# Moving the norms' squares and sums between engines, filling TensorE's gaps, and splitting one weight block later, in a two-layer RG-LRU / GLA step

## The chip, the cores and the metric

The kernel runs on one core of a Trainium2 chip. The metric is the device time of one execution in microseconds (us). The engines are named as the profile names them: PE (TensorE, matmuls; PEld is its weight load), DVE (VectorE), ACT (ScalarE), POOL (GpSimd) and SP (SyncE, which here only issues DMAs). They run side by side and meet through semaphores.

## The reference, cut to what matters

Two groups of tokens (128 context tokens, 256 sample tokens; 384 in all) pass through two layers. Each layer is: half FFN, mixer (RG-LRU in layer 0, GLA in layer 1), half FFN. Each of these six stages begins with a modulated RMS norm, and a seventh norm ends the program:

```python
def rms_norm(x, g):
    y = xf * rsqrt(mean(xf * xf, axis=-1) + EPS)        # over 1024 features
    return y * g
def modulated(x, mod, gains, j):
    return rms_norm(x, gains[j]) * (1.0 + mod[3*j+1]) + mod[3*j]
def half_ffn(x, ...):                                   # w_in 1024 x 5632, w_out 2816 x 1024
    g, u = split(modulated(x, ...) @ w_in)
    return x + 0.5 * mod[3*j+2] * ((silu(g) * u) @ w_out)
# layer i: half_ffn, x += mod[5] * mixer(modulated(x)), half_ffn;   mod = silu(c) @ ada_w[i] + ada_b[i]
y = rms_norm(x, final_norm)
```

All is float32. The weights (some 250 MB) are read once.

## The kernel before, in words

**Layout.** x lies in SBUF as 8 chunks of 128 features (partitions) by 384 tokens. A matmul with float32 precision is made of three fp32r matmuls: high part of the weight by high part of the activation, high by low, low by high (L557 to L559 in `tile`). A weight block is up to 11 tiles of 128 x 128. It comes by DMA into `raw` (a ring of 4 slots, SP), ACT copies it to `w_hi_sb` (`hi_of`, L868), and DVE subtracts to get `w_lo_sb` (`lo_of`, L1242). `ahead(n)` does this for block n + 4. The semaphore `w_split` counts finished splits, and the load of block n + 4 into the slot waits for the split of block n.

**Stages.** `ffn_in` has 44 blocks of 8 tiles (24 matmuls each), `ffn_out` 16 blocks of 11 tiles (33 matmuls each, two blocks for one chunk of x), `rg_out` 8 blocks of 10 tiles, `gla_out` 8 blocks of 8 tiles. In the out stages, DVE adds each finished chunk to x (`update_x`, L1409, semaphore `x_ready`). In the FFN stages of the first three FFNs it also computes the modulation rows, called ada here: two multiply-and-sum passes over 128 x 1024 for each block of `ada_w` (L1261 and L1264), whose loads POOL issues into a ring of 2.

**A norm (q = 0 to 6).** While the stage before still runs, POOL squares chunks 0 to 6 of x and sums them into `ss` (`sum_squares`, L480 to L483). When chunk 7 is updated, ACT squares it into `sq_last` (L881) and loads the table for the square root (L882). PE sums over the partitions with `ones` as the moving operand, six matmuls with one column each (L575, L576), ACT takes the root (L884), DVE the reciprocal (L1293) and multiplies it with the identity into `diag` (L1294). PE multiplies `ones` with `diag`, which spreads the factor over all partitions (`rinv`, L584). Then for each chunk DVE scales (`scaled`, L1323), ACT adds the shift and rounds to the high part (L893), and DVE makes the low part (`low`, L1331).

**The start of a stage.** The first four blocks of a stage run in `arriving`: for chunks 0 to 4 all four blocks take the chunk as it arrives (8 matmuls with the high part, L595 and L596, then 4 with the low part, L599), and chunks 5 to 7 follow block by block. All four blocks must be split before the first matmul.

**The prologue.** SP loads small inputs, two pairs of ada blocks (1 MB each pair), all of x in one DMA, six more pairs, and the first four weight blocks. PE computes 7 of these 16 ada blocks, DVE 9. Then come norm 0, four `hi_of`, four `lo_of`, and the first stage. The masks for GLA are loaded from ACT's queue here.

The order of all of this is the order in which the code of each engine is written. There is no scheduler.

## Time and profile before

| | |
|---|---|
| median of 3 runs | 1612.21 us (1610.89 to 1615.01) |
| the profiled execution | 1613.05 us, of which the span from first to last instruction is 1611.4 us |
| busy share of the span | PE 94%, DVE 72%, ACT 39%, POOL 20% |
| mean granted TensorE clock | 0.970 of full |
| chain that ended last | PE 75%, DVE 11%, issue 5%, ACT 4%, POOL 3%, DMA 2% |

A row of the timeline is: start in us, duration in us, engine, line, operation, out<-in, shape, count, and in brackets the idle time before it and what ended it. Matmuls overlap, so that the time from one start to the next is what one costs.
### The profile page before, as it was taken

What the parts mean: (1) busy time and instruction counts of PE and PEld (TensorE: products, weight loads), DVE (VectorE), ACT (ScalarE), POOL (GpSimd) and SP (SyncE); (2) the same over time, 40 slices, a digit from 0 to 9 for tenths busy, and PEclk for the clock granted to TensorE, in tenths of its full rate; (3) what the DMA queues carried; (4) which work ended last, traced back from release to release, by engine and by line L of the source; (5) the groups of instructions that cost most, each with busy time, mean ns of one, the idle gap of its engine ahead of it and who ended that gap; (6) DMA issues with size and microseconds to landing.
All of it is one profiled execution on the core that took longest, in us unless ns stands there. A gap on an engine that the chain in (4) does not pass through costs nothing.

```text
span 1611.4 us, 24129 instructions
## 1 busy us (share of the span) xinstructions
PE 1520.8 (94%) x8554; PEld 1490.4 (92%) x8554; DVE 1164.8 (72%) x1691; ACT 634.7 (39%) x883; POOL 325.4 (20%) x377
## 2 busy tenths in 40 slices
PE   6899999989978999999899999989989889999997
PEld 5899999979978999999899999989779789999997
DVE  6898889878987777789977777986766665434432
ACT  1533342259973333332333333225444444333321
POOL 5010002300244000014200000321567240000031
PEclk9999999989988999999899999999999899999998
DMA  8476676513423556666455556652212133333421
GB/s 335 168 245 232 212 248 220 197 59 105 148 69 131 192 186 195 199 212 235 161 171 194 186 197 209 220 209 66 92 65 80 40 105 119 129 128 130 158 92 39
DMA packets 67909, 257.00 MB, mean 159 GB/s; under 512 B 7537, under 2 KB 8561, under 8 KB 67473
## 3 DMA queue, kind: packets, MB, share of 16 engines
q1 hardware_dynamic: 48512, 187.57, 34.0%
q0 software_dynamic: 18432, 67.12, 12.6%
q10 hardware_dynamic: 912, 1.65, 0.3%
q8 instruction: 28, 0.46, 0.1%
q14 instruction: 25, 0.20, 0.0%
HBM read 253.68 MB, written 2.63 MB: 159 GB/s over the span
## 4 chain that ended last, share of the span: by engine, by line
PE 75%; DVE 11%; issue 5%; ACT 4%; POOL 3%; DMA 2%; SPq 0%; DVEq 0%; ACTq 0%; POOLq 0%
PE bank L557 21%; PE bank L559 21%; PE bank L558 21%; DVE wide L1261 3%; DVE wide L1264 3%; PE bank L595 2%; PE bank L596 2%; PE bank L599 2%; ACT w_hi_sb L868 1%; PE wide L766 1%; DMA ada_raw<-in_ada_w 1%; DVE w_lo_sb L1242 1%; DMA x<-in_x 1%; DVE x L1409 1%; POOL scr L483 1%
## 5 line engine op out<-in xcount | busy, mean ns | idle before, releaser
L868 ACT ACTIVATE w_hi_sb<-raw 128x1024 fp32r<-128x1024 f32 (+3 forms) x308 | 344.1, 1122 | 535.4 <-PE bank L559 524.6
L557 PE MATMUL bank<-h_hi,w_hi_sb 128*128 128x384 f32 x1620 | 546.7, 337 | 3.8 <-DVEq L1804 3.0
L1242 DVE TENSOR_TENSOR w_lo_sb<-raw,w_hi_sb 128x1024 fp32r<-128x1024 f32 (+3 forms) x308 | 427.0, 1388 | 168.3 <-ACT w_hi_sb L868 163.9
L559 PE MATMUL bank<-h_hi,w_lo_sb 128*128 128x384 f32 x1620 | 544.9, 336 | 0.0
L558 PE MATMUL bank<-h_lo,w_hi_sb 128*128 128x384 f32 x1620 | 544.9, 336 | 0.0
L557 PEld LDWEIGHTS bank<-h_hi,w_hi_sb 128*128 128x128 f32 x1620 | 305.1, 188 | 6.3 <-DVEq L1804 3.2
L558 PEld LDWEIGHTS bank<-h_lo,w_hi_sb 128*128 128x128 f32 x1620 | 305.1, 188 | 0.1
L559 PEld LDWEIGHTS bank<-h_hi,w_lo_sb 128*128 128x128 f32 x1620 | 305.0, 188 | 0.0
L557 PE MATMUL bank<-a_hi,w_hi_sb 128*128 128x384 f32 x704 | 237.0, 337 | 2.5 <-DVE a_lo L1390 1.5
L559 PE MATMUL bank<-a_hi,w_lo_sb 128*128 128x384 f32 x704 | 236.6, 336 | 0.0
L558 PE MATMUL bank<-a_lo,w_hi_sb 128*128 128x384 f32 x704 | 236.6, 336 | 0.0
L1261 DVE CUSTOM_DVE_ANT_0 wide<-ada_raw,extra 128x1024 f32<-128x1024 f32 x128 | 171.8, 1342 | 8.1 <-DMA ada_raw<-in_ada_w 7.8
L1264 DVE CUSTOM_DVE_ANT_0 wide<-ada_raw,extra 128x1024 f32<-128x1024 f32 x128 | 157.8, 1233 | 4.4
L458 POOL DMA_DIRECT2D ada_raw<-in_ada_w x80 | 42.6, 532 | 553.0 <-DVE mod_turn L1264 508.0
L557 PEld LDWEIGHTS bank<-a_hi,w_hi_sb 128*128 128x128 f32 x704 | 132.3, 188 | 3.7 <-issue 3.7
L558 PEld LDWEIGHTS bank<-a_lo,w_hi_sb 128*128 128x128 f32 x704 | 132.4, 188 | 0.0
L559 PEld LDWEIGHTS bank<-a_hi,w_lo_sb 128*128 128x128 f32 x704 | 132.4, 188 | 0.0
L910 ACT ACTIVATE tmp_b<-bank 128x384 f32<-128x384 f32 x88 | 43.2, 491 | 207.8 <-PE bank L559 207.8
L1379 DVE TENSOR_TENSOR tmp_a<-tmp_b,bank 128x384 f32<-128x384 f32 x88 | 48.8, 555 | 100.7 <-PE bank L559 97.9
L483 POOL TENSOR_TENSOR scr<-scr 128x384 f32<-128x384 f32 x42 | 77.4, 1843 | 3.3
L595 PE MATMUL bank<-h_hi,w_hi_sb 128*128 128x384 f32 x140 | 54.7, 391 | 14.8 <-ACT h_hi L893 14.8
L465 POOL DMA_DIRECT2D ada_raw<-in_ada_w x48 | 26.5, 552 | 171.0 <-DVE mod_all L1264 164.9
(263 smaller groups left out, 1616.3 us busy)
## 6 DMA issues: line engine op xcount, KB each, us to landing
raw<-in_ffn_in SPq DMA_DIRECT2D x176, 512.0 KB, 3.6
ada_raw<-in_ada_w POOLq DMA_DIRECT2D x128, 512.0 KB, 3.6
raw<-in_ffn_out SPq DMA_DIRECT2D x64, 704.0 KB, 4.2
...
```

The source lines that it names most:

```text
L458: pool.dma_start(ada_raw[:, b, :], d["ada_w"][bass.ds(ADA_RING * i + (first + b), 1)].rearrange("a p k -> p (a k)")).then_inc(ada_loaded[b ...
L483: add = nc.gpsimd.tensor_tensor(ss[:, :], ss[:, :], sq[:, :], ALU.add)
L557: pe.matmul(out, w_hi_sb[:, slot, w], hi[k], start=start and j == 0, stop=False)
L558: pe.matmul(out, w_hi_sb[:, slot, w], lo[k], start=False, stop=False)
L559: last = pe.matmul(out, w_lo_sb[:, slot, w], hi[k], start=False, stop=stop and j == len(ks) - 1)
L595: pe.matmul(bank[b][:, 0:T], w_hi_sb[:, b, w], chunks[0][k], start=k == 0, stop=False)
L868: A(w_hi_sb[:, s, 0:w], raw[:, s, 0:w], ACT.Copy).then_inc(w_hi, 1)
L910: A(tmp_b[:, p, 0:T], bank[2 * p][:, 0:T], ACT.Silu).then_inc(silu_ready, 1)
L1242: V.tensor_tensor(w_lo_sb[:, s, 0:w], raw[:, s, 0:w], w_hi_sb[:, s, 0:w].bitcast(F32), ALU.subtract).then_inc(w_split, 1)
L1261: V.tensor_tensor_reduce(wide[:, :], w, crow[:, 0, :], 1.0, 0.0, ALU.mult, ALU.add, accum_out=out[:, 0:1]).then_inc(ada_half, 1)
L1264: V.tensor_tensor_reduce(wide[:, :], w, crow[:, 1, :], 1.0, 0.0, ALU.mult, ALU.add, accum_out=out[:, 1:2]).then_inc(done, 1)
L1379: V.tensor_tensor(tmp_a[:, two, :], tmp_b[:, two, :], bank[2 * two + 1][:, 0:T], ALU.mult).then_inc(drained, 2)
```

## The change

Eight things change.

- The squares of chunks 0 to 6 move from POOL to ACT (`square`), and the additions into `ss` move to DVE (`add_square`). In an FFN's out stage ACT squares chunk m after it has split block 2m + 5, and DVE adds after the same block's low part. POOL keeps only its DMA issues and the work inside the mixers.
- The column sums come in two parts: three matmuls with `ss` before the wait for `sq_last`, three behind it.
- `diag` is gone. PE takes the factor itself, broadcast along columns, as the stationary operand and the identity as the moving one (three matmuls of 128 columns, fp32).
- `keep_busy(n)`: n matmuls of `ones` by `ident` into an unused bank, whose result nobody reads. There are 4 before the second part of the sums, 5 behind it, and 9 behind the spreading, the 9 not in norms 0 and 6, and none at all in norm 0.
- The table of the root is loaded before the wait for chunk 7.
- The last of the four first blocks of a stage is split inside the norm, behind chunk 4 (`LATE`), and `arriving` runs three blocks by chunks (chunks 0 to 6), then the fourth as a whole.
- Prologue: x comes in 8 pieces, one behind each pair of ada blocks, the masks behind the fourth piece and on SP's queue; ACT makes three of the four high parts before the root; DVE makes the first low part before the reciprocal and two behind it.
- POOL issues its 16 ada loads of an out stage in one run. `wg2` is loaded behind norm 4's last chunk.

```diff
 def sum_squares(q, loads=None):                       # POOL: all of it is removed
-    ...
@@ TensorE
+def keep_busy(n):
+    for _ in range(n):
+        pe.matmul(bank[7][:, 0:P], ones[:, :], ident, start=True, stop=True)
 def norm_sums(q):
-    pe.wait_ge(ss_ready, q + 1)
+    pe.wait_ge(sq_added, (DC - 2) * (q + 1))
     ...
+    for t in range(NT):
+        pe.matmul(sum_ps[:, t:t + 1], ss[:, t * P:(t + 1) * P], ones[:, 0:1], start=t == 0, stop=False)
+    if q:
+        keep_busy(4)
     pe.wait_ge(sq_ready, q + 1)
     for t in range(NT):
-        pe.matmul(sum_ps[:, t:t + 1], ss[:, tok], ones[:, 0:1], start=True, stop=False)
         last = pe.matmul(sum_ps[:, t:t + 1], sq_last[...], ones[:, 0:1], ...)
 def norm(q):
     if q:
         norm_sums(q)
-    pe.wait_ge(diag_ready, q + 1)
-    pe.matmul(rinv, ones[:, :], diag[...], start=True, stop=True).then_inc(rinv_ready, 1)
+        keep_busy(5)
+    pe.wait_ge(factor_ready, q + 1)
+    for t in range(NT):
+        last = pe.matmul(rinv[:, t * P:(t + 1) * P], rstd[:, t:t + 1].to_broadcast([P, P]), ident, ...)
+    last.then_inc(rinv_ready, 1)
+    if 0 < q < 6:
+        keep_busy(9)
-def arriving(base, ks, chunks, hi_ready, ready, n0, early=5, bank=bank):
+def arriving(base, ks, chunks, hi_ready, ready, n0, early=5, bank=bank, together=RING):
     ...                                               # RING -> together in all loops
+    for b in range(together, RING):
+        pe.wait_ge(w_split, base + b + 1)
+        tile(bank[b][:, 0:T], b, ks, *chunks, True, True).then_inc(w_used, 1)
-    one_tile_blocks(f"ffn_in{f}", ..., DC * q)
+    one_tile_blocks(f"ffn_in{f}", ..., DC * q, DC - 1, RING - 1)       # also rg and gla_qk
@@ ScalarE
 def norm_stats(q):
     ...
+    nc.scalar.preload_act_table_set("sqrt_and_others")
+    if q:
         act.wait_ge(x_ready, DC * q)
     A(sq_last[:, :], x[:, DC - 1, :], ACT.Square).then_inc(sq_ready, 1)
-    nc.scalar.preload_act_table_set("sqrt_and_others")
+    if q == 0:
+        for n in range(RING - 1):
+            hi_of(n)
 def norm_apply(q, tables):
     ...
+        if q and m == LATE:
+            ahead(BASE[STAGE_BEFORE[q]] + COUNT[STAGE_BEFORE[q]] - 1)
+        if q == 0 and m == LATE:
+            hi_of(RING - 1)
-def only_weights(name):
-    for b in range(COUNT[name]):
+def only_weights(name, q=None, per=1):
+    for b in range(COUNT[name] - 1):
         ahead(BASE[name] + b)
+        if q and b % per == per - 1 and b // per < DC - 1:
+            square(q, b // per)
@@ VectorE
 def norm_stats(q):
-    seq.step(V.reciprocal(rstd[:, 0:NT], rstd[:, 0:NT]))
-    V.tensor_tensor(diag[:, :, :], ident..., rstd..., ALU.mult).then_inc(diag_ready, 1)
+    V.reciprocal(rstd[:, 0:NT], rstd[:, 0:NT]).then_inc(factor_ready, 1)
+def add_square(q, m):
+    dve.wait_ge(sq_made, (DC - 1) * q + m + 1)
+    if m > 1:
+        dve.wait_ge(sq_added, (DC - 2) * q + m - 1)
+    V.tensor_tensor(ss[:, :], ss[:, :], sq[:, :], ALU.add).then_inc(sq_added, 1)
@@ SyncE, prologue
 for s in range(ADA_START // 2):
-    if s == 2:
-        sp.dma_start(x[:, :, :], d["x"]).then_inc(x_loaded, 16)
     sp.dma_start(ada_first[:, 2 * s:2 * s + 2, :], ...)
+    sp.dma_start(x[:, s, :], d["x"][:, s, :]).then_inc(x_loaded[s], 16)
+    if s == 3:
+        sp.dma_start(mask_in, d["masks"]).then_inc(masks_loaded, 16)
```

How the order on the engines changes is shown at three places. The first is PE between the last matmul of `ffn_out0` and the first of the mixer (norm 1); `scr` is the buffer that holds `ss`, `sq_last` and `diag`, and `small` holds the identity. Before:

```order
L559 MATMUL bank<-a_hi,w_lo_sb 128x384
L619 REGISTER_ALU
L619 COMPARE_AND_BRANCH
L575 MATMUL bank<-ones,scr 128x1
L576 MATMUL bank<-ones,scr 128x1
L575 MATMUL bank<-ones,scr 128x1
L576 MATMUL bank<-ones,scr 128x1
L575 MATMUL bank<-ones,scr 128x1
L576 MATMUL bank<-ones,scr 128x1
L584 MATMUL bank<-scr,ones 128x384
L595 MATMUL bank<-h_hi,w_hi_sb 128x384
```

And the same place in the changed kernel:

```order
L537 MATMUL bank<-a_hi,w_lo_sb 128x384
L613 REGISTER_ALU
L613 COMPARE_AND_BRANCH
L556 MATMUL bank<-ones,scr 128x1 x3
L548 MATMUL bank<-small,ones 128x128 x4
L561 MATMUL bank<-ones,scr 128x1 x3
L548 MATMUL bank<-small,ones 128x128 x5
L572 MATMUL bank<-small,rstd 128x128 x3
L548 MATMUL bank<-small,ones 128x128 x9
L586 MATMUL bank<-h_hi,w_hi_sb 128x384
```

The sums stand in two groups, and 18 matmuls that nobody waits for are queued between the steps of the norm.

The second place is DVE inside norm 3 of the changed kernel, around chunk 4 (L1336 scales, L1344 makes the low part, L1258 is the low part of a weight block):

```order
L1344 SCALAR_TENSOR_TENSOR h_lo<-tmp_a,mod_all,h_hi 128x128
L1344 SCALAR_TENSOR_TENSOR h_lo<-tmp_a,mod_all,h_hi 128x256
L1258 TENSOR_TENSOR w_lo_sb<-raw,w_hi_sb 128x1024
L1336 SCALAR_TENSOR_TENSOR tmp_a<-x,gain,bank 128x128
L1336 SCALAR_TENSOR_TENSOR tmp_a<-x,gain,bank 128x256
L1344 SCALAR_TENSOR_TENSOR h_lo<-tmp_a,mod_all,h_hi 128x128
L1344 SCALAR_TENSOR_TENSOR h_lo<-tmp_a,mod_all,h_hi 128x256
```

Before, that low part of a weight block stood ahead of the reciprocal, and the chunks followed one another without it.

The third place is DVE in `ffn_out1`, behind the update of a chunk (L1433 updates x, L1277 is an ada pass), in the changed kernel:

```order
L1433 SCALAR_TENSOR_TENSOR x<-bank,halfgate,x 128x128
L1433 SCALAR_TENSOR_TENSOR x<-bank,halfgate,x 128x256
L1258 TENSOR_TENSOR w_lo_sb<-raw,w_hi_sb 128x1024
L1428 TENSOR_TENSOR scr<-scr 128x384
L1277 ISA wide,mod_all<-ada_raw,extra 128x1024
```

The addition of a chunk's squares (L1428) is new there, between the low part and the ada pass.

## Rows read from the trace of the kernel before

**Rows 1.** Stretches: us, busy time (count) by engine, granted clock, DMA share, GB/s

```profile
0.00:49.80 49.80, 28.39 (x126) 27.10 (x126) 35.20 (x50) 12.67 (x16) 22.50 (x23) 1.00 0.82 316
...
22.00:26.00 4.00, 4.00 (x20) 4.00 (x20) 3.82 (x5) 0.00 (x0) 3.83 (x3) 1.00 1.03 410
...
503.70:511.60 7.90, 3.20 (x16) 2.03 (x15) 4.32 (x11) 5.28 (x8) 0.00 (x0) 0.69 0.64 228
1077.10:1088.60 11.50, 4.56 (x17) 3.17 (x15) 6.70 (x17) 5.60 (x9) 0.00 (x0) 0.63 0.53 194
1088.60:1314.80 226.20, 208.87 (x1168) 191.89 (x1168) 151.98 (x217) 103.24 (x166) 110.33 (x133) 0.94 0.23 75
```

**Rows 2.** Timeline across norm 2, PE, ACT and DVE

```profile
503.75 0.74 DVE L1409 SCALAR_TENSOR_TENSOR x<-bank,mod_all,x 128x128 f32<-128x128 f32 x2 [2.40 <-PE bank L559]
...
504.77 0.51 ACT L881 ACTIVATE scr<-x 128x384 f32<-128x384 f32 x1
...
505.29 1.28 ACT L882 ACT_TABLE_LOAD   x1
505.42 0.35 PE L575 MATMUL bank<-ones,scr 128*128 128x1 f32 x2 [1.71 <-ACT scr L881]
...
506.97 0.26 ACT L884 ACTIVATE rstd<-bank,eps 128x3 f32<-128x3 f32 x1 [0.40 <-PE bank L576]
...
507.48 0.56 DVE L1294 TENSOR_TENSOR scr<-small,rstd 128x384 f32<-128x384 f32 x1
...
508.09 1.65 PE L584 MATMUL bank<-scr,ones 128*128 128x384 f32 x2 [1.16 <-DVE scr L1294]
509.85 1.39 DVE L1323 SCALAR_TENSOR_TENSOR tmp_a<-x,gain,bank 128x128 f32<-128x128 f32 x4 [1.73 <-PE bank L584]
...
511.57 0.66 PE L595 MATMUL bank<-h_hi,w_hi_sb 128*128 128x384 f32 x1 [1.83 <-ACT h_hi L893]
```

**Rows 3.** Timeline, PE inside GLA: six fp32 matmuls of 128 columns, two passes each

```profile
1205.84 1.50 PE L766 MATMUL wide<-ebuf 128*128 128x128 f32 x12
```

**Rows 4.** First matmul of a stage to the clock's rise, first of five and sum

```profile
335.10:339.90 4.80, 4.79 (x16) 4.80 (x17) 4.69 (x14) 2.63 (x8) 0.00 (x0) 0.55 0.02 3
...
sum 26.30, PE 26.25 PEld 26.29 DVE 25.70 ACT 14.73 POOL 0.00; mean PE 5.25 PEld 5.26 DVE 5.14 ACT 2.95 POOL 0.00
```

**Rows 5.** Timeline, DVE: low parts of two chunks in norm 2, one in norm 4

```profile
514.33 0.74 DVE L1331 SCALAR_TENSOR_TENSOR h_lo<-tmp_a,mod_all,h_hi 128x128 fp32r<-128x128 f32 x2
...
515.76 0.74 DVE L1331 SCALAR_TENSOR_TENSOR h_lo<-tmp_a,mod_all,h_hi 128x128 fp32r<-128x128 f32 x2
...
1090.13 0.97 DVE L1331 SCALAR_TENSOR_TENSOR h_lo<-tmp_a,mod_all,h_hi 128x128 fp32r<-128x128 f32 x2
```

**Rows 6.** Timeline, DVE in the out stage of the third FFN

```profile
1049.66 2.42 DVE L1242 TENSOR_TENSOR w_lo_sb<-raw,w_hi_sb 128x1408 fp32r<-128x1408 f32 x1 [0.15 <-DVE x L1409]
1052.01 2.04 DVE L1261 CUSTOM_DVE_ANT_0 wide<-ada_raw,extra 128x1024 f32<-128x1024 f32 x1
...
1055.29 1.62 DVE L1242 TENSOR_TENSOR w_lo_sb<-raw,w_hi_sb 128x1408 fp32r<-128x1408 f32 x1
...
1079.18 0.74 DVE L1409 SCALAR_TENSOR_TENSOR x<-bank,halfgate,x 128x128 f32<-128x128 f32 x2
```

**Rows 7.** Groups of instructions: busy us, mean ns of one, idle before

```profile
L1390 DVE TENSOR_TENSOR a_lo<-tmp_a,a_hi 128x384 f32 x80 | 44.3, 554 | 0.0
```

**Rows 8.** Timeline of the prologue, DVE

```profile
9.29 1.23 DVE L1261 CUSTOM_DVE_ANT_0 wide<-ada_first,extra 128x1024 f32<-128x1024 f32 x1 [9.29 <-DMA ada_first<-in_ada_w]
...
21.29 1.73 DVE L1261 CUSTOM_DVE_ANT_0 wide<-ada_first,extra 128x1024 f32<-128x1024 f32 x1
...
40.67 1.23 DVE L1264 CUSTOM_DVE_ANT_0 wide<-ada_first,extra 128x1024 f32<-128x1024 f32 x1
...
43.58 4.63 DVE L1242 TENSOR_TENSOR w_lo_sb<-raw,w_hi_sb 128x1024 fp32r<-128x1024 f32 x4
...
48.13 1.38 DVE L1323 SCALAR_TENSOR_TENSOR tmp_a<-x,gain,bank 128x128 f32<-128x128 f32 x4
```

136 lines of the change are left out of this document (67 added, 69 removed).

## The prediction, made before the changed kernel was run

> **What bounds the kernel now.** I read the engines' shares first: PE is busy for 94% of the span, so the kernel is one stream of matmuls with holes. The table of stretches shows where the holes are. The first 49.8 us hold no matmul of a stage [rows 1], and between two stages PE's weight matmuls pause for some 8 us five times (7.9 us at norm 2), with 11.5 us at norm 4 [rows 1]; a seventh pause ends the program. Third, the timeline across one norm shows the pause as a chain over three engines [rows 2]: x's last chunk, ACT's square, PE's sums, root, reciprocal, diagonal, spreading, scaling, first matmul. Nothing there is throughput. Fourth, the granted clock: it is 0.69 over that pause [rows 1] and still 0.55 in the first 4.8 us of the stage behind norm 1 [rows 4]. So each pause costs twice, once as waiting and once as matmuls at 1.2 GHz. Inside the stages PE hardly waits; what DVE, ACT and POOL do there is free unless it is late at the stage's end.
>
> **The chain of a norm, by norm 2** [rows 2].
> - ACT starts the last square at 504.77, since a `hi_of` stands before it; x is ready at 503.75 + 0.74 = 504.49. Without the `hi_of` it starts at 504.54: 0.23 us earlier, at 504.54, done at 505.05.
> - The sums: six matmuls from 505.42, root at 506.97, so 1.55 us. A matmul here is two passes, and two passes of one column last 0.22 us in start-to-start time (twelve passes in 1.44). Three of the six go before the wait. Behind it stand 0.66 us, so 0.67 to 0.9 us are saved; I take 0.89.
> - What stands before the wait must not be late: 3 sums (0.66) and 4 fillers. One fp32 matmul of 128 columns costs 2 x (1.50 - 0.27)/11 = 0.22 us at full clock [rows 3]; together 1.55 us from 503.54, so PE is free at 505.1, and the square reaches PE at 505.2. They fit, by 0.1 us.
> - The root and the reciprocal take 0.11 + 0.26 + 0.04 + 0.18 us. The diagonal (0.56 us and a hand-over) goes: 0.6 us saved. But 5 fillers (1.1 us) are queued behind the sums, in front of the spreading, and the factor is there after about 0.7 us. So 0.4 us of the gain are given back.
> - The spreading cost 1.65 us, at the low clock. Three matmuls of 128 columns are 6 x 0.111 + 0.17 = 0.83 us at full clock: 0.8 us saved (at half clock 1.45: 0.2 saved).
> - From scaling to first matmul 1.72 us, unchanged; 9 fillers (2.0 us from the spreading's last issue) end at about the same moment.
> Sum: 0.23 + 0.89 + 0.6 - 0.4 + 0.8 = 2.1 us; going through the times one by one gives 2.0. Norms 3 and 5 have the same chain, norm 1 slightly slower sums: 2.4, 2.0, 1.9 us for norms 1, 2, 5.
>
> **DVE's lateness.** Norm 4's pause is 11.5 us because DVE updates the last chunk only at 1079.18 [rows 6], 2 us after PE's last matmul at 1077.1. In that stage a POOL tensor instruction makes DVE's pass of 1.62 us last 2.42 and its pass of 1.23 us last 2.04 [rows 6, 8]: 1.6 us for each chunk. That goes; an addition of 0.55 us [rows 7] comes, with ACT's square finished beneath the low part. So DVE wins 1.0 us for each of seven chunks and is on time: about 1.7 us at norm 4 and 0.3 to 0.5 at norm 3. Norm 4's chain gives 3.3 more, since its pause is so long that six sums run at the low clock (0.43 us each, 1.2 us more than at norm 2). I take 5.0 at norm 4 and 2.3 at norm 3. ACT's seven squares of 0.51 us lie beneath PE in a stage where ACT is busy for a third. Bound on the other side: if the additions made DVE wait for ACT by 1 us each, DVE would be as late as now and 2 us of this are lost.
>
> **The end.** Norm 6 has the same chain without the last fillers: 0.7 + 0.6 - 0.4 + 0.8 = 1.6 us.
>
> **The clock.** Five stages begin with 26.3 us in all at a granted clock near 0.54 [rows 4], 16 matmuls in the first of them and 88 in the five, that would take 0.173 us each at full clock (15.2 us): 11.1 us lost. If the fillers keep the clock up, this is gained. But then PE can be faster than the chunks arrive. Three blocks take 9 x 0.173 = 1.56 us a chunk; DVE delivers one in 1.43 us [rows 5] and so stays ahead, until the late low part (1.23 us) comes in behind chunk 4. Following both engines chunk by chunk I get waits of 0.3 us at chunk 5 and 0.4 at chunk 7: 0.7 us. In norm 4 the chunks are rearranged, a low part takes 0.97 instead of 0.74 [rows 5], a chunk 1.65, which is slower than PE's 1.56: some 2.6 us of waits. 4 x 0.7 + 2.6 = 5.4 us come off: net 5.7 us. Before, with four blocks (2.08 us a chunk), DVE never was the limit.
>
> The bounds of this term: 11.1 us from above, and from below the case where the clock falls all the same (rival 1). The rows show that PE at work is not enough: within norm 2 the pieces of idle time are 1.7, 1.2 and 1.8 us with sums between them, and the clock falls. The sums move one column each. A filler moves 128 columns in two passes back to back, like GLA's matmuls, in whose stage the granted clock is 0.94 [rows 1]. So I take "held".
>
> The table load before the root ends at 505.29 + 1.28 = 506.57 [rows 2], before the sums do; it costs nothing now, and would be 0.4 us late behind the shorter sums if it were not moved. The Trainium skill (ScalarE: Activation LUTs, "What ACT_TABLE_LOAD costs") gives a load with its drain as 2.66 us. By that the root could not have begun before 507.95, and moving it would win 1.0 us more per norm, 6 us in all. The trace does not agree: the root begins at 506.97. The measurement decides, and this is no part of the sum.
>
> **The prologue** [rows 1, 8]. DVE starts its 9 ada blocks at 9.3 and is through at 41.9, with one wait for the transfer of all of x. With POOL at work one pass lasts 1.73 instead of 1.23 us. Now a block costs two passes with their readout, 2 x 1.38 = 2.76 us, and six additions 0.6 us each with their hand-over: 9 x 2.76 + 3.6 = 28.4, so 37.8. The DMA keeps up: 410 GB/s bring a pair of blocks and a piece of x (1.25 MB) in 3.04 us against DVE's 3.36; the last pair lands near 31.6, the last piece of x at 32.1. ACT has squared it and made three high parts (1.06 us each, the third when its load lands, near 36) by 37.1, the root by 37.4. DVE makes one low part (1.16 us), reciprocal, mods, gain, two low parts, and starts scaling at 42.4 instead of 48.13: 5.7 us. The fourth low part is hidden, as PE starts at the low clock. Before, this first stage ran only 3.4 us at the low clock until it rose; the other five took 5.3 on average [rows 4]. I count the average here, 1.9 us more at the low clock, of which almost half is lost: 0.9 to 1.0 us. 4.7 us net, between 3 (DMA pieces of 1.5 KB rows slower than before, by no row) and 6.5.
>
> **The sum.** Prologue 4.7; chains 2.4 + 2.0 + 2.3 + 5.0 + 1.9 + 1.6 = 15.2; clock 5.7: 25.6 us. From the profiled execution's 1613.05: 1587.4. The median is 0.84 lower; 1587.
>
> **Rivals.**
> 1. The clock falls in the pauses all the same. Then the fillers cost double: 5 of them 2.1 us against 0.7 needed, 9 of them 3.8 against 1.7, so 3.6 us of overrun against 1.7 us saved. But 9 fillers and the spreading are continuous work just ahead of the stage, and the clock comes back earlier, by up to the 2.2 us that a stage loses now. The five norms together give nothing, except DVE's 2 us at norms 3 and 4; with the prologue and norm 6: 1606. If it falls in two or three of five: 1597. For it: the fit before the second sums has a margin of 0.1 us only, and PE is idle or in one-column work for 1.3 of each pause. Against: the 18 fillers are 4 us of the 6 us.
> 2. DVE's chunk chain starves PE more than I follow, since each hand-over between ACT and DVE behind the late block is exposed: 1.5 us more at five stages, 1594 to 1595. For it: 1.43 against 1.56 us is a thin lead.
> 3. Slower than before: the fillers themselves. If the clock falls and the 9 fillers do not bring it back, each of five pauses is 1.9 us longer (9.5), the stages begin as cold as now, and only the prologue and norm 6 are won (5.7 together); if the small DMAs of x and DVE's later additions take the prologue's gain too, nothing stands against 9.5: 1613 to 1621. It decides from the point where the clock is low in all five pauses when the second group of fillers starts.
> 4. The additions hold DVE up in the out stages. Only norms 3 and 4 could tell: 2 us less, inside the range.
>
> **How the numbers follow.** Forecast as worked out 0.70; rival 1 0.15, of which a third beyond 1605; rival 2 0.10; rival 3 0.05. Likeliest 1587, its own range 1582 to 1592. The range reaches to partly lost clocks: 1579 to 1600. About 0.3% (4.8 us) can be told from no change. Faster by more: 0.70 + 0.10 + 0.12 = 0.92; within: 0.05; slower: 0.03.
>
> **What would show it.** Scaling of norm 0 at 42.4. Each pause, last matmul to first weight matmul, near 6 us, norm 4's 6.5. Granted clock 1.00 there and no 0.32 us matmul spacing behind. PE waits of below 1 us behind chunk 4, more in norm 4. DVE's passes all at 1.23 and 1.62 us in the out stages, x's last chunk 0.4 us behind PE at norm 4. Wrong would be: a clock of 0.5 at any stage start, PE busy with fillers when `rstd` has long been ready, or a longer wait of PE for `w_lo_sb` of the fourth block.

## The result and the profile after

| | median of the runs | profiled span | mean granted clock | PE busy |
|---|---|---|---|---|
| before | 1612.56 us (1610.89 to 1615.01, 4 runs) | 1611.4 us | 0.970 | 94% |
| changed | 1586.07 us (1584.52 to 1588.69, 4 runs) | 1585.4 us | 0.987 | 96% |

The ratio is 0.9834, with a 95% interval from 0.9820 to 0.9848: 26 us faster. The prediction was 1587 us.

The stretches of the changed kernel (columns as in [rows 1]: length, then busy time and count of PE, PEld, DVE, ACT and POOL, then granted clock, DMA share and GB/s): prologue, first stage, pause of norm 1, RG-LRU stage, pause of norm 2, pause of norm 4.

```profile
0.00:44.10 44.10, 28.32 (x130) 27.98 (x131) 31.06 (x54) 15.04 (x21) 2.15 (x10) 1.00 0.89 345
44.10:321.40 277.30, 276.80 (x1584) 276.50 (x1585) 239.32 (x364) 99.98 (x132) 24.38 (x46) 1.00 0.63 217
321.40:327.50 6.10, 6.10 (x55) 6.08 (x54) 2.38 (x8) 2.86 (x6) 0.00 (x0) 1.00 0.00 0
327.50:492.70 165.20, 150.99 (x843) 148.34 (x843) 144.75 (x244) 132.64 (x204) 31.99 (x32) 0.96 0.36 118
492.70:498.90 6.20, 6.20 (x56) 6.18 (x55) 2.45 (x9) 2.99 (x6) 0.00 (x0) 1.00 0.05 19
...
1061.00:1067.50 6.50, 6.43 (x57) 6.25 (x55) 2.86 (x11) 3.28 (x7) 0.00 (x0) 1.00 0.00 1
```

Beside [rows 1], the pause of norm 2 is 6.2 us with PE busy throughout at a granted clock of 1.00; it was 7.9 us with 3.2 us of work at 0.69. The pause of norm 4 went from 11.5 to 6.5 us. One row is misleading. The granted clock also says 1.00 for the first stage, although its first matmuls start 0.32 us apart, against 0.173 us at full clock; there, in the first microseconds of the program, the distance of the starts is the better witness.

The timeline across norm 2, to be set beside [rows 2]:

```profile
493.02 0.74 DVE L1433 SCALAR_TENSOR_TENSOR x<-bank,mod_all,x 128x128 f32<-128x128 f32 x2 [2.35 <-PE bank L537]
493.41 1.14 PE L548 MATMUL bank<-small,ones 128*128 128x128 f32 x8
493.80 0.52 ACT L881 ACTIVATE scr<-x 128x384 f32<-128x384 f32 x1 [3.14 <-DVE x L1433]
494.38 0.82 PE L561 MATMUL bank<-ones,scr 128*128 128x1 f32 x6
495.07 1.36 PE L548 MATMUL bank<-small,ones 128*128 128x128 f32 x10
495.24 0.26 ACT L886 ACTIVATE rstd<-bank,eps 128x3 f32<-128x3 f32 x1 [0.92 <-PE bank L561]
...
495.54 0.18 DVE L1309 RECIPROCAL rstd<-rstd 128x3 f32<-128x3 f32 x1 [1.77 <-ACT rstd L886]
...
496.26 0.83 PE L572 MATMUL bank<-small,rstd 128*128 128x128 f32 x6
```

ACT squares 0.04 us after x is there, the sums behind the square take 0.82 us (three matmuls) instead of 1.55 (six), the spreading 0.83 instead of 1.65. No PE row has an idle time in brackets: the fillers (L548; x8 is four of them, two passes each) close the gaps. They also hold the spreading up. The reciprocal starts at 495.54 and takes 0.18 us, and PE comes to L572 only at 496.26, behind five fillers (L548, x10).

Set out by the first and last weight matmul of each stage, the 26.0 us of span are:

| | before | after | won |
|---|---|---|---|
| first matmul of the first stage | 49.84 | 44.11 | 5.7 |
| pauses of norms 1 to 5 | 8.70, 8.20, 8.46, 11.62, 8.08 | 6.28, 6.28, 6.27, 6.53, 6.21 | 13.5 |
| from the last weight matmul to the end | 12.83 | 11.22 | 1.6 |
| stages 1 to 6 | 276.57, 168.26, 277.71, 279.23, 225.88, 276.02 | 277.26, 165.00, 275.61, 280.15, 225.65, 274.83 | 5.2 |

### The profile page after: what moved, and what is told of

The parts are those of the page before. It is cut to its first block, busy times and chain, and to the rows that moved or that the text cites. A ratio compares the mean times of both kernels' runs of the same rounds, so it can differ in the third digit from the quotient of the medians.

```text
span 1585.4 us, 24611 instructions
## 1 busy us (share of the span) xinstructions
PE 1525.6 (96%) x8780; PEld 1501.9 (95%) x8780; DVE 1139.2 (72%) x1726; ACT 655.5 (41%) x932; POOL 193.4 (12%) x286
## 4 chain that ended last, share of the span: by engine, by line
PE 85%; DVE 5%; ACT 3%; POOL 2%; issue 2%; DMA 2%; SPq 1%; POOLq 0%; DVEq 0%; ACTq 0%
PE bank L535 25%; PE bank L537 24%; PE bank L536 24%; PE bank L586 1%; PE bank L587 1%; PE bank L590 1%; PE bank L548 1%; DMA ada_first<-in_ada_w 1%; PE wide L759 1%; ACT w_hi_sb L861 1%; DMA ada_raw<-in_ada_w 1%; DVE w_lo_sb L1258 1%; POOL ebuf L523 1%; DVE wide L1280 1%; DVE wide L1277 1%
## 5 line engine op out<-in xcount | busy, mean ns | idle before, releaser
L1258 DVE TENSOR_TENSOR w_lo_sb<-raw,w_hi_sb 128x1024 fp32r<-128x1024 f32 (+3 forms) x308 | 404.4, 1314 | 170.0 <-ACT w_hi_sb L861 166.7
L1277 DVE CUSTOM_DVE_ANT_0 wide<-ada_raw,extra 128x1024 f32<-128x1024 f32 x128 | 157.1, 1227 | 9.4 <-DMA ada_raw<-in_ada_w 9.1
L1280 DVE CUSTOM_DVE_ANT_0 wide<-ada_raw,extra 128x1024 f32<-128x1024 f32 x128 | 157.8, 1233 | 4.4
L463 POOL DMA_DIRECT2D ada_raw<-in_ada_w x80 | 42.6, 533 | 604.5 <-DVE mod_turn L1280 523.2
L926 ACT ACTIVATE a_hi<-tmp_a 128x384 f32 (+1 forms) x88 | 45.2, 513 | 30.1 <-DVE tmp_a L1396 30.1
L895 ACT ACTIVATE h_hi<-tmp_a,mod_all 128x128 fp32r<-128x128 f32 x96 | 39.6, 468 | 34.4 <-DVE tmp_a L1336 34.4
```

Source lines behind the costliest of these rows:

```text
L463: pool.dma_start(ada_raw[:, b, :], d["ada_w"][bass.ds(ADA_RING * i + (first + b), 1)].rearrange("a p k -> p (a k)")).then_inc(ada_loaded[b ...
L926: A(out, tmp_a[:, p, 0:T], ACT.Copy).then_inc(ahi_ready, 1)
L1258: V.tensor_tensor(w_lo_sb[:, s, 0:w], raw[:, s, 0:w], w_hi_sb[:, s, 0:w].bitcast(F32), ALU.subtract).then_inc(w_split, 1)
L1277: V.tensor_tensor_reduce(wide[:, :], w, crow[:, 0, :], 1.0, 0.0, ALU.mult, ALU.add, accum_out=out[:, 0:1]).then_inc(ada_half, 1)
L1280: V.tensor_tensor_reduce(wide[:, :], w, crow[:, 1, :], 1.0, 0.0, ALU.mult, ALU.add, accum_out=out[:, 1:2]).then_inc(done, 1)
```

## The experiments

The median of the kernel before, run beside them, was 1612.51 us for no_fill, together4, pool_loop and pool_squares, 1611.56 for the next four rows and 1613.31 for the last four. The pauses and the length of the third stage (us) are from one execution, the profiled one, of each; a pause goes from the start of the last weight matmul to the start of the next stage's first, a stage from its first to its last.

| | median (range, runs) | ratio to before, 95% interval | pauses of norms 1 to 5 | 3rd stage |
|---|---|---|---|---|
| changed kernel | 1586.07 (1584.5 to 1588.7, 4) | 0.9834 (0.9820 to 0.9848) | 6.28 6.28 6.27 6.53 6.21 | 275.61 |
| no_fill | 1592.50 (1590.6 to 1594.5, 4) | 0.9870 (0.9852 to 0.9887) | 5.88 5.88 5.87 6.84 5.80 | 277.55 |
| together4 | 1614.78 (1605.3 to 1619.1, 12) | 1.0007 (0.9990 to 1.0024) | 7.93 9.56 9.55 8.18 9.49 | 277.51 |
| pool_loop | 1585.90 (1582.5 to 1586.7, 5) | 0.9827 (0.9812 to 0.9842) | 6.27 6.29 6.27 6.53 6.22 | 275.61 |
| pool_squares | 1587.99 (1585.6 to 1593.2, 5) | 0.9840 (0.9826 to 0.9854) | 6.28 6.28 6.26 9.69 6.21 | 275.62 |
| together4_by5 | 1599.15 (1596.0 to 1603.7, 6) | 0.9920 (0.9906 to 0.9935) | 7.93 7.93 11.02 8.18 9.49 | 275.24 |
| mid_by7 | 1595.12 (1594.7 to 1599.8, 4) | 0.9892 (0.9878 to 0.9906) | 6.21 6.21 6.24 6.70 6.22 | 277.51 |
| mid_by5 | 1583.96 (1580.7 to 1589.7, 5) | 0.9826 (0.9808 to 0.9845) | 6.21 6.22 6.24 6.69 6.21 | 275.24 |
| with_diag | 1585.60 (1583.7 to 1587.4, 5) | 0.9836 (0.9824 to 0.9849) | 6.46 6.46 6.46 6.71 6.39 | 275.61 |
| fill3 | 1584.39 (1581.9 to 1586.8, 5) | 0.9817 (0.9804 to 0.9831) | 5.89 5.89 5.89 6.14 5.82 | 275.61 |
| warm0 | 1584.36 (1582.7 to 1586.8, 5) | 0.9819 (0.9806 to 0.9832) | 6.28 6.28 6.28 6.54 6.21 | 275.61 |
| first_four | 1589.64 (1584.2 to 1594.2, 5) | 0.9843 (0.9824 to 0.9861) | 6.29 6.29 6.27 6.53 6.21 | 275.59 |
| combined | 1582.43 (1579.0 to 1583.0, 5) | 0.9806 (0.9792 to 0.9819) | 6.02 6.02 6.25 6.69 5.82 | 275.22 |

**no_fill: the fillers alone taken out.**

```diff
-                for _ in range(n):
+                for _ in range(0):
                     pe.matmul(bank[7][:, 0:P], ones[:, :], ident, start=True, stop=True)
```

> The changed kernel without its fillers (keep_busy issues nothing); all else as changed. Theory A (the fillers hold TensorE's clock, and that is worth what the stages' starts lost before): the granted clock falls to 0.5 in all five pauses between stages, the spreading of the factor costs 1.45 instead of 0.83 us, but starts up to 0.4 us earlier; the five stages begin at the low clock as in the kernel before, about 11 us lost there, less the waits behind the late split (they vanish under slow matmuls, about 3 us). Time 1586 + 8 = 1592 to 1596, ratio to the kernel before 0.987 to 0.990. Rival B (the split sums and the shorter chain alone keep the pause short enough): clock stays at 1.0, the 0.4 us that the second group of fillers holds up each norm come back: 1584, ratio 0.982.

Measured 1592.5 us, 6.4 above the changed kernel. The first 4.6 us of the third stage, and below them the pause of norm 2 that stands before it:

```profile
502.60:507.20 4.60, 4.56 (x14) 4.59 (x15) 4.49 (x14) 2.44 (x7) 0.00 (x0) 0.50 0.01 4
496.80:502.60 5.80, 2.62 (x20) 2.25 (x18) 2.44 (x9) 2.97 (x6) 0.00 (x0) 0.85 0.04 18
```

The pause is 0.40 us shorter without fillers, but the clock falls inside it, and the stage's first 4.6 us run at 0.50. The third stage is 1.9 us longer (277.55 against 275.61), the last one 2.3. So at such a norm the fillers cost 0.4 us and bring about 2. The intervals of the two ratios do not touch. The stretch of the changed kernel behind the same norm shows that it held:

```profile
498.90:511.40 12.50, 12.46 (x72) 12.05 (x72) 10.85 (x29) 6.62 (x16) 0.00 (x0) 1.00 0.13 43
```

**together4: the late split undone in norms 1 to 5, fillers kept.** All four first blocks run chunk by chunk up to the seventh chunk.

```diff
-                arriving(..., DC - 1, bank, RING - 1)         # norms 1 to 5
+                arriving(..., DC - 1, bank, RING)
-                    if q and m == LATE:
-                        ahead(BASE[STAGE_BEFORE[q]] + COUNT[STAGE_BEFORE[q]] - 1)
-                for b in range(COUNT[name] - 1):              # and the same for DVE
+                for b in range(COUNT[name]):
```

> The changed kernel with the late split undone in norms 1 to 5: all four first blocks are split before the norm, and the four take each chunk together (as before, chunks 0 to 6 together); fillers kept. Norm 0 keeps its late split. Theory A (with the clock up, the late low part makes TensorE wait for chunks, so the late split costs time): TensorE needs 2.08 us a chunk against DVE's 1.43 and never waits; 0.8 us come back at norms 1 to 3 and 5 and 2.2 at norm 4, against 0.23 to 0.28 us that ACT's extra high part delays the last square at each of five norms: net 3 us faster, 1583, ratio 0.9815. Rival B (the late split is worth more than it costs, since a high part in front of the last square moves the whole chain and shifts it against the fillers): 1587 to 1589, ratio 0.985.

Measured 1614.78 us: all of the gain gone, and every theory's number missed by 25 us or more. The profile shows two faults. The first is in the pause, here of norm 2:

```profile
501.18 0.74 DVE L1429 SCALAR_TENSOR_TENSOR x<-bank,mod_all,x 128x128 f32<-128x128 f32 x2 [2.35 <-PE bank L537]
501.24 1.06 ACT L861 ACTIVATE w_hi_sb<-raw 128x1024 fp32r<-128x1024 f32 x1 [3.73 <-PE bank L537]
...
502.32 1.28 ACT L878 ACT_TABLE_LOAD   x1
...
503.61 0.52 ACT L881 ACTIVATE scr<-x 128x384 f32<-128x384 f32 x1
504.19 0.83 PE L561 MATMUL bank<-ones,scr 128*128 128x1 f32 x6 [1.48 <-ACT scr L881]
504.88 2.45 PE L548 MATMUL bank<-small,ones 128*128 128x128 f32 x10
```

The copy of the last block must wait for PE's last matmul, and the table load and the last square are queued behind it on ACT. The square starts at 503.61, 1.69 us after x is there, instead of 0.04. PE is idle for 1.48 us, the clock falls, and the ten passes of five fillers take 2.45 us instead of 1.36, in front of the spreading. So a filler can also do harm: once the clock is low it costs twice, on the chain. The late split is not there for DVE alone; it is what lets the table load stand ahead of x's last chunk. The second fault comes some 20 us behind four of the five pauses (not behind norm 4's), and the next runs take it apart. The pauses of the profiled execution, one of the faster of the twelve with 1609.9 us, add up to 13.1 us more than the changed kernel's; where the slower ones lost 5 us more is not known.

Here the Trainium skill can be weighed (ScalarE: Activation LUTs, "What ACT_TABLE_LOAD costs": 2.66 us with the drain). In these rows the load starts when the copy ends and takes 1.28 us, and the square starts 1.29 us after the load's start. The trace does not agree with the longer figure here.

**together4_by5, mid_by7, mid_by5: the two faults apart.** together4_by5 keeps the copy where together4 has it. `by5` lets the chunk-by-chunk part end at the fifth chunk, as before the change. `mid` splits the last block in the pause, but behind the last square on ACT and behind the reciprocal on DVE.

```diff
-                arriving(..., DC - 1, bank, RING - 1)
+                arriving(..., 5, bank, RING)                 # by5; DC - 1 in by7
                 A(sq_last[:, :], x[:, DC - 1, :], ACT.Square).then_inc(sq_ready, 1)
+                if 0 < q < 6:                                # mid; DVE alike, ahead of norm_apply
+                    ahead(BASE[STAGE_BEFORE[q]] + COUNT[STAGE_BEFORE[q]] - 1)
```

> The four first weight blocks together as in the run before last (together4, 1614.8 us), but chunk by chunk only up to the fifth chunk of h, the last three chunks block by block, as the kernel before had it. Theory S (slots): with all four blocks taken chunk by chunk up to the seventh, their slots come free only at the end and within 2 us of each other, so the fifth block's halves (ACT 1.06 us, then DVE 1.23 us) are late; that is the wait of 2.3 to 2.7 us for w_lo_sb behind each of the five pauses, with a half-speed stretch behind it. Here these waits vanish, and the pauses stay at 7.9 to 9.6 us because the fourth block's copy by ACT is still queued ahead of the table load and the last square: 1598 to 1603 us. Rival R: the stages are longer because they start cold behind the longer pauses, and the waits are a consequence: 1611 to 1615.

> The last block of a stage is split in the pause itself, but out of the way: ACT copies it behind the last square, DVE takes its low part behind the reciprocal; then four blocks chunk by chunk up to the seventh. Theory Q (queue) says that the pauses' extra 1.65 to 3.3 us in together4 came from the copy ahead of the table load and the last square, so they are 6.3 to 6.5 us here. Theory S says that the wait for the fifth block's low part (2.3 to 2.7 us, five times) stays: 1595 to 1604 us. If four blocks by seven chunks were harmless in themselves: 1583 to 1586.

> As mid_by7, with the chunk-by-chunk part up to the fifth chunk only. Q and S together: pauses of 6.3 to 6.5 us, no wait for the fifth block, and no wait for h_lo behind a late split (1.2 us at norm 4); against that up to 1 us a norm where PE is at the sixth chunk ahead of DVE (4 x 5 x 3 x 0.173 = 10.4 us of work against 8 chunks at 1.44). 1584 to 1589 us, that is: the changed kernel's time without its late split. If the late split of three blocks is needed in itself: over 1592.

| third stage / pause before it | up to chunk 7 | up to chunk 5 |
|---|---|---|
| copy ahead of the square | 277.51 / 9.56 | 275.24 / 7.93 |
| copy behind the square | 277.51 / 6.21 | 275.24 / 6.22 |

The medians landed where both theories together put them, mid_by5 at the edge (1583.96, 1584 to 1589 expected). The number of chunks sets the stage. The place of the copy sets the pause, but by how much hangs on the clock. Where it holds, the copy ahead of the square costs 1.65 us: 7.93 against 6.28, and 8.18 against 6.53 at norm 4. Where it falls, copy and clock together cost 3.3 us, and 4.8 at norm 3 in together4_by5 (11.02, above the 9.6 that I expected). Norm 2 in together4_by5 has the same 1.48 us of idle time as in together4, and its fillers run at full clock:

```profile
498.96 0.83 PE L561 MATMUL bank<-ones,scr 128*128 128x1 f32 x6 [1.48 <-ACT scr L881]
499.65 1.36 PE L548 MATMUL bank<-small,ones 128*128 128x128 f32 x10
```

So 9.56 against 7.93 in the first row of the table is the clock, and not the chunks. The second fault in mid_by7, behind norm 2:

```profile
519.74 0.49 ACT L916 ACTIVATE tmp_b<-bank 128x384 f32<-128x384 f32 x1 [5.95 <-PE bank L537]
520.13 1.99 ACT L861 ACTIVATE w_hi_sb<-raw 128x1024 fp32r<-128x1024 f32 x2
521.21 1.23 DVE L1258 TENSOR_TENSOR w_lo_sb<-raw,w_hi_sb 128x1024 fp32r<-128x1024 f32 x1 [6.64 <-ACT w_hi_sb L861]
522.57 0.56 DVE L1396 TENSOR_TENSOR tmp_a<-tmp_b,bank 128x384 f32<-128x384 f32 x1
...
523.26 0.44 PE L535 MATMUL bank<-h_hi,w_hi_sb 128*128 128x384 f32 x1 [2.00 <-DVE tmp_a L1396]
```

ACT had been idle for 5.95 us and DVE for 6.64, since no block was finished; then four finish within some 2 us, and PE waits for what the two must do with the first: a split into its slot, and the emptying of its bank. PE waited for `tmp_a` behind norms 2, 3 and 5 (2.0 us each), for `w_lo_sb` behind norm 1 (2.7 us), and for neither behind norm 4: four waits, not the five of the expectation. In the changed kernel the held-back fourth block is PE's work in that time. My expectation named the slot alone; the banks are as much of it.

mid_by5 has neither fault nor a late split. Its third stage is 0.37 us shorter than the changed kernel's, its last 0.34. The first 96 weight matmuls of a stage are its four first blocks. The time from the first to the last of them shows the cost where it arises, apart from what happens later in the stage:

| first 96 weight matmuls, us | behind norm 1 | 2 | 3 | 4 | 5 |
|---|---|---|---|---|---|
| changed (three blocks by 7 chunks, late split) | 16.93 | 16.93 | 16.93 | 18.60 | 16.91 |
| mid_by5 (four blocks by 5 chunks) | 16.57 | 16.56 | 16.56 | 18.16 | 16.57 |
| mid_by7 (four blocks by 7 chunks) | 16.57 | 16.55 | 16.55 | 16.56 | 16.57 |

Without any wait they take 16.56 us. So beside mid_by5 the late split costs 0.34 to 0.37 us, and 0.44 behind norm 4. Behind norm 4, where DVE's chunks come more slowly [rows 5], mid_by5 loses 1.6 us as well, though I had expected no such wait there:

```profile
1077.98 0.44 PE L535 MATMUL bank<-h_hi,w_hi_sb 128*128 128x384 f32 x1 [1.31 <-DVE h_lo L1346]
```

The median of mid_by5, 1583.96, is not distinguishable from 1586.07.

**pool_squares: squares and sums of norms 1 to 6 back on POOL.**

```diff
+                    seq.step(nc.gpsimd.tensor_tensor(sq[:, :], x[:, m, :], x[:, m, :], ALU.mult))
+                    nc.gpsimd.tensor_tensor(ss[:, :], ss[:, :], sq[:, :], ALU.add).then_inc(sq_added, 1)
...
-                        square(q, b // per)                  # ACT
-                        add_square(norm_q, b)                # DVE
```

> The changed kernel with squares and sums of norms 1 to 6 back on POOL as before (norm 0 stays on ACT and DVE), its ada loads interleaved as before; split sums, fillers, spreading and late split kept. Theory A (moving the squares only matters by POOL slowing DVE): passes of DVE beside POOL last 2.04 instead of 1.23 us and 2.42 instead of 1.62, DVE updates the last chunk 2 us late at norm 4 and 0.5 us at norm 3, nothing at the others: 2 to 3 us slower than the changed kernel, 1588 to 1589, ratio 0.985 to 0.9855; with the pause longer by 2 us at norm 4, the clock may fall there and take 2 us more, 1591. Rival B (POOL's sums are late for the first part of the column sums, at every norm): 1 us or more at each of six norms, 1593 or more. Rival C: no difference, 1586.

The median, 1587.99, is where theory A had it, but the intervals overlap, and it cannot be told from the changed kernel's. The pauses can: only norm 4's changes, 9.69 us instead of 6.53, and DVE's low parts in the stage before it are long again. From pool_squares, then from the changed kernel:

```profile
1046.22 2.43 DVE L1274 TENSOR_TENSOR w_lo_sb<-raw,w_hi_sb 128x1408 fp32r<-128x1408 f32 x1 [0.15 <-DVE x L1449]
...
1065.20 0.74 DVE L1449 SCALAR_TENSOR_TENSOR x<-bank,halfgate,x 128x128 f32<-128x128 f32 x2
```

```profile
1039.92 1.62 DVE L1258 TENSOR_TENSOR w_lo_sb<-raw,w_hi_sb 128x1408 fp32r<-128x1408 f32 x1 [0.73 <-ACT w_hi_sb L861]
...
1061.33 0.74 DVE L1433 SCALAR_TENSOR_TENSOR x<-bank,halfgate,x 128x128 f32<-128x128 f32 x2 [0.82 <-PE bank L537]
```

The last update has no wait in the first: DVE is late, 2.23 us behind the start of PE's last matmul instead of 0.38. In the second it waits for PE. That is 1.85 of the 3.16 us. The rest is the clock, which falls here behind 1.68 us of idle time and makes the spreading and the nine fillers slow (0.67 and 0.61 us), as the expectation had allowed for:

```profile
1066.55 0.83 PE L579 MATMUL bank<-ones,scr 128*128 128x1 f32 x6 [1.68 <-ACT scr L899]
...
1068.46 1.49 PE L590 MATMUL bank<-small,rstd 128*128 128x128 f32 x6
```

At norm 3 nothing is seen (6.26 against 6.27). In the kernel before, DVE was 0.92 us behind PE there, in pool_squares it waits for PE. So POOL's squares alone do not bring that lateness back, and what took it away stays open.

**with_diag: the factor spread as before the change** (reciprocals on a diagonal by DVE, one matmul of 384 columns), fillers kept.

```diff
+                V.tensor_tensor(diag[:, :, :], ident..., rstd[:, 0:NT]..., ALU.mult).then_inc(factor_ready, 1)
-                for t in range(NT):
-                    last = pe.matmul(rinv[:, t * P:(t + 1) * P], rstd[:, t:t + 1].to_broadcast([P, P]), ident, ...)
+                pe.matmul(rinv, ones[:, :], diag..., start=True, stop=True).then_inc(rinv_ready, 1)
```

> The factor is spread as before the change: DVE puts the reciprocals on a diagonal (0.56 us in the kernel before) and one matmul of 384 columns with ones spreads it, instead of three of 128 columns with the identity; all fillers stay. Theory: the diagonal lies on the chain, so each of six pauses is 0.4 to 0.6 us longer, 2.4 to 3.6 us in all: 1588.5 to 1590. Rival: PE is held by its ten fillers for most of that time anyway (they end 0.7 us behind the reciprocal), so only 0.1 to 0.2 us a pause is seen: 1586.5 to 1587.5.

The rival was right: pauses of 6.46 instead of 6.28, and a median of 1585.60 us that cannot be told from the changed kernel's. The step that took 0.56 us on DVE [rows 2] is hidden, but for 0.18 us, behind the five fillers. In norm 0, which has none, the same step costs 0.6 us: from the start of the last sum to the spreading it is 3.73 against 3.14 us.

**fill3: three fillers instead of five ahead of the spreading.**

```diff
-                    keep_busy(5)
+                    keep_busy(3)
```

> Five keep-alive matmuls of 128 columns behind the first part of the column sums become three. The five take 1.14 us on PE and end 0.1 to 0.4 us behind the last square of ACT, which the second part of the sums waits for. Theory: each pause is 0.3 to 0.4 us shorter (6.28 to 5.9) and the clock still holds: 1584 to 1585 us, which a median may not tell from the changed kernel; the pauses tell it. Rival: with two fillers fewer the clock falls in the pause and the stage starts at half speed, 1 to 2 us a stage: 1590 to 1595.

(The expectation puts the five behind the first part of the sums; they stand behind the second.) The pauses are 5.89 us, as short as with no fillers at all, and the stages as long as with five (275.61, 274.85), so the clock held. The median, 1584.39 us, cannot be told from the changed kernel's (the intervals overlap); the pauses and stages show the 0.39 us a norm.

**warm0: twelve fillers in norm 0.**

```diff
+                else:
+                    keep_busy(6, 3)            # ahead of the spreading, in bank 3
...
+                if q == 0:
+                    keep_busy(6, 3)            # behind it
```

> Norm 0, which has no fillers in the changed kernel, gets six ahead of and six behind the spreading of the factor (into a bank that is free there), in the two stretches of 2.79 and 2.80 us in which PE waits. The changed kernel's first stage runs 4.5 us at half clock (44.11 to 48.58). Theory: the clock is up at or soon behind the start, and 1 to 2.2 us are won: 1584 to 1585 us, the first stage 275.1 to 276.3 us long instead of 277.3. Rival: at half clock twelve fillers take 0.44 us each, delay the spreading or the first matmul, and the clock still rises only with the stage: 1586 to 1588, the stage as long as now.

All but its first matmul start at the spacing of the full clock, and the stage is 275.61 us long instead of 277.26, as the first theory said:

```profile
45.84 0.42 PE L590 MATMUL bank<-h_hi,w_hi_sb 128*128 128x384 f32 x1 [2.08 <-ACT h_hi L899]
46.09 0.34 PE L591 MATMUL bank<-h_hi,w_lo_sb 128*128 128x384 f32 x1
46.27 0.33 PE L590 MATMUL bank<-h_hi,w_hi_sb 128*128 128x384 f32 x1
```

In the changed kernel the same matmuls start 0.32 us apart:

```profile
44.57 0.53 PE L587 MATMUL bank<-h_hi,w_lo_sb 128*128 128x384 f32 x1
44.89 0.53 PE L586 MATMUL bank<-h_hi,w_hi_sb 128*128 128x384 f32 x1
45.21 0.53 PE L587 MATMUL bank<-h_hi,w_lo_sb 128*128 128x384 f32 x1
```

The start itself, 45.84, is 1.7 us later in this execution. The loads of the prologue come in at different times: with an unchanged prologue the start lay between 44.11 (changed) and 45.27 (pool_squares) in nine kernels. That the fillers do not hold it up is seen in combined, which has the same twelve and starts at 44.42. The medians do not decide here.

**first_four: the first stage's late split undone.**

```diff
-                    for n in range(RING - 1):
+                    for n in range(RING):
                         hi_of(n)
-            for b in range(1, RING - 1):
+            for b in range(1, RING):
                 lo_of(b)
```

> The first stage's late split undone: ACT and DVE split all four first weight blocks ahead of norm 0's scaling, and PE takes four blocks chunk by chunk up to the fifth chunk of h; the rest of the prologue's change stays. Theory: DVE has one low part more (1.15 us) on the chain, so the scaling starts at 43.5 to 43.7 us from the span's start instead of 42.40, and of this 0.5 to 0.7 comes back because the first stage then loses no 0.7 us to the late split (277.3 us long, 276.6 before the change): 1586 to 1587.5 us. Rival: the 0.7 us is not the split's but the half clock's (4.5 us of it instead of 3.3), so the stage stays 277.3 us long and the whole 1.15 is lost: 1587 to 1588.

From the reciprocal to the scaling it is 4.49 us instead of 2.96, and the root before it is late as well. The DVE rows, of first_four and then of the changed kernel:

```profile
41.01 3.50 DVE L1256 TENSOR_TENSOR w_lo_sb<-raw,w_hi_sb 128x1024 fp32r<-128x1024 f32 x3
44.42 1.38 DVE L1334 SCALAR_TENSOR_TENSOR tmp_a<-x,gain,bank 128x128 f32<-128x128 f32 x4
```

```profile
40.12 2.36 DVE L1258 TENSOR_TENSOR w_lo_sb<-raw,w_hi_sb 128x1024 fp32r<-128x1024 f32 x2
42.40 1.38 DVE L1336 SCALAR_TENSOR_TENSOR tmp_a<-x,gain,bank 128x128 f32<-128x128 f32 x4
```

The scaling starts 2.0 us later, more than both theories gave it. The low part is 1.14 us of this. The rest goes with ACT's fourth copy, which waits for its block until 38.69 and puts the root at 39.65 instead of 38.36. The stage did not get shorter, it is 278.06 us: on the stage the rival was right. The length of the first stage follows the time that its matmuls start 0.32 us apart, of which 0.46 is lost (1 - 0.173/0.32), and in these five nothing else is seen:

| | before | changed | mid_by5 | first_four | fill3 |
|---|---|---|---|---|---|
| stage length | 276.57 | 277.26 | 277.73 | 278.06 | 276.54 |
| at half clock | 2.96 | 4.30 | 5.52 | 6.20 | 2.69 |
| length less 0.46 of it | 275.2 | 275.3 | 275.2 | 275.2 | 275.3 |

How long it lasts differs where the change has no hand in it. With the late split or without it the rest is the same, so a slow start hides the late split; warm0, which starts warm, is 275.61 us long and not 275.2, as the other stages with a late split (0.37 us). The median of 1589.64 (1584 to 1594) is above both theories, but its interval overlaps with the changed kernel's. Its profiled run also has long second, fourth and fifth stages (167.43, 280.42, 227.25). None of them points at the edit: pool_squares, warm0 and the changed kernel have lengths within 0.3 us of these (167.65, 227.3 and 280.15).

**pool_loop: the sixteen loads of an out stage issued by a loop.** In the changed kernel PE waits in the third FFN's out stage. Its PE row, and the POOL rows just before:

```profile
990.99 0.68 PE L535 MATMUL bank<-a_hi,w_hi_sb 128*128 128x384 f32 x1 [2.87 <-DVEq L1452]
```

```profile
973.37 0.53 POOL L470 DMA_DIRECT2D ada_raw<-in_ada_w  x1 [2.06 <-DVE mod_all L1280]
981.00 0.54 POOL L470 DMA_DIRECT2D ada_raw<-in_ada_w  x1 [7.10 <-issue]
```

```diff
-                for n in range(n_ada, n_ada + ADA_OUT):
-                    ada_load(n)
+                ada_run(n_ada, ADA_OUT)
```

> The changed kernel with POOL's 16 ada loads of each out stage issued from a loop instead of one after another in straight code. In the changed kernel's trace POOL stands still for 7.1 us in its own program (no releaser) before the second load of the third FFN's out stage; DVE then waits 5.0 us for that load, TensorE 2.9 us for DVE (1.0 us in the kernel before), and the clock falls for 3.4 us behind it. Theory A (the stall is POOL fetching its straight code): with a loop it is gone there, TensorE does not wait, the clock stays up: 2.9 + 1.6 = 3 to 4.5 us faster, 1582, ratio 0.981. Rival B (the load is late for another reason, such as the DMA or semaphores): POOL still stands 6 to 7 us, time unchanged, 1586, ratio 0.9834. Rival C: the stall moves to another place in POOL's program, where it is hidden or not: between the two.

```profile
980.74 0.54 POOL L463 DMA_DIRECT2D ada_raw<-in_ada_w  x1 [6.12 <-issue]
```

Rival B was right: the stall is still there, now inside the loop, and 1585.90 us is no difference. It is there in all fourteen traces. In eight it lasts 5.9 to 6.2 us, the kernel before, with_diag and pool_loop among them (6.07, 6.02 and 6.12), and PE's wait behind it is at most 1.0 us. In six it lasts 6.8 to 7.2 us (the changed kernel, pool_squares, fill3, mid_by7, first_four and combined), and PE waits 1.3 to 3.4 us. The clock falls behind this wait in the three with the longest:

| | stall | PE's wait | clock behind it | fourth stage |
|---|---|---|---|---|
| mid_by5 | 6.03 | 0.73 | held | 276.24 |
| pool_loop | 6.12 | 0.79 | held | 276.69 |
| fill3 | 7.14 | 1.82 | held | 277.72 |
| changed | 7.10 | 2.87 | fell | 280.15 |
| first_four | 6.93 | 2.96 | fell | 280.42 |
| mid_by7 | 7.20 | 3.43 | fell | 283.97 (its second fault in it) |

What POOL does in these microseconds the trace doesn't show, and why it is at times 1 us longer stays open.

**combined: mid_by5, pool_loop, fill3 and warm0 together.**

> What came out at or below the changed kernel, together: the last block split in the pause (ACT behind the last square, DVE behind the reciprocal) with four blocks by five chunks, POOL's sixteen loads of an out stage issued by a loop, three fillers instead of five, and fillers in norm 0. If the parts add: 1586.1 - 1.2 (no wait for h_lo at norm 4) - 6 x 0.35 (fillers) - 1 to 2 (norm 0) - 0 to 3 (the wait at half clock in the third FFN) = 1578 to 1582 us. Rival: the earlier copy on ACT takes the slack that the shorter pauses count on and they stay 6.2 us: 1581 to 1584.

1582.43 us (interval of the ratio 0.9792 to 0.9819) against 0.9820 to 0.9848 for the changed kernel: the lowest median of all, 0.3% below the changed kernel by the ratios, with two intervals that just do not touch. It overlaps with the intervals of fill3, warm0 and mid_by5, so it cannot be told from those. The first stage runs at full clock (275.62), but the pauses are 6.02, 6.02 and 6.25, not 5.85. The rival's time (1581 to 1584) was right, its reason was not: the root follows the last square by 1.44 us in fill3 and in combined alike, so ACT's copy delays nothing. What delays the chain is DVE's low part between the reciprocal and the scaling. From spreading to scaling it is 1.15, 1.13, 1.36 and 1.57 us at norms 1 to 4, and 1.00 at each in fill3.

## Why the prediction was right, step by step

- **The prologue.** Scaling starts at 42.40, as worked out, but by two errors that cancel: DVE was through with its ada blocks at 38.4 us, not 37.8, and what stands between them and the scaling took 4.0 us instead of 4.6. In the other kernels with this prologue it starts between 42.4 and 43.6. The longer time at half clock, which I took as 1.0 us, was 0.7 (0.69 us of stage length). The reason that I gave was only an average, and the 3.4 us that I read for the kernel before are 3.0 by the distance of the starts; the runs show 0 to 6.2 us of it, by chance or by fillers.
- **The chains.** 2.4, 2.0, 2.3, 5.0, 1.9 and 1.6 us were predicted; 2.4, 1.9, 2.2, 5.1, 1.9 and 1.6 came. At norm 2 the shares are: last square earlier 0.24 (0.23 predicted), sums 0.77 (0.89), reciprocal to spreading 0.09 (0.6 less 0.4), spreading 0.81 (0.8). That the five fillers give back 0.4 is shown by no_fill and fill3. But the gain of the diagonal and their price are not two separate terms: with five fillers in the way, taking the diagonal out wins 0.18 us. No run takes back the sums in two parts, the earlier table load or the new order of the prologue's loads; their shares are read from the timelines.
- **DVE's lateness.** Shown by pool_squares: DVE is 1.85 us late at norm 4, where I gave it 1.7, and the clock that falls with it makes 3.2. At norm 3, where I gave it 0.3 to 0.5, the pause shows nothing.
- **The clock, "held".** Shown by no_fill. The pauses have a granted clock of 1.00, and rivals 1 and 3 did not happen. Nor did rival 2, by the next point, nor rival 4, as DVE updates the last chunk 0.38 us behind PE's last matmul at norm 4.
- **Waits behind the late split, 5.4 us.** This term was too large. Beside mid_by7, in which PE does not wait over the first four blocks, the changed kernel loses 0.34 to 0.38 us in them at four norms, not 0.7, and 2.0 at norm 4, not 2.6: 3.5 us in all. At norm 4 most of it is not the late split's, since mid_by5 loses 1.6 us there too. The waits of the changed kernel there:

```profile
1077.60 0.79 PE L590 MATMUL bank<-h_lo,w_hi_sb 128*128 128x384 f32 x3 [0.81 <-DVE h_lo L1344]
1080.42 0.45 PE L535 MATMUL bank<-h_hi,w_hi_sb 128*128 128x384 f32 x1 [0.38 <-DVE h_lo L1344]
```

- **What I did not see.** Two things that are in no term nearly cancel the 1.9 us by which the last one was too large. The fourth stage is 3.9 us longer than in mid_by5 (280.15 against 276.24), through the wait of 2.87 us shown above and 3.4 us at half clock behind it; the kernel before has this wait with 1.00 us and no fall of the clock, so that some 3.6 us of it are new (1.9 of wait, and half of 3.4). And the second stage won 3.3 us where 1.7 were due (2.0 for the clock, less 0.36). In both kernels PE waits 2.96 us for ACT in it (until 363.19 in the kernel before, until 354.12 in the changed one); before, the clock falls behind this wait, in the changed kernel it does not. Its length is 165.0 us in three of these kernels and 166.0 to 171.9 in the others. So that 1587 stands so near to 1586.07 is also luck: the waits 1.9 us too pessimistic, 1.6 us won in the second stage, 3.6 lost in the fourth.
- **The purpose of the late split.** I priced it as a cost of the change, and the expectation of together4 took its absence for free. together4 shows that, without it, this order loses everything. The step that fails there is that four blocks by seven chunks would run like three: I had counted PE's and DVE's pace chunk by chunk, and not when slots and banks come free.
